# A longer ring for gathered V rows, U slots released by twos and a third index buffer in a PEER block on one core

## What is computed

```python
def _peer(h, w_peer_q, peer_sub_keys, peer_u, peer_v):
    q = (h @ w_peer_q).reshape(B, S, PEER_HEADS, 2, PEER_HALF)
    s = jnp.einsum('bshcd,hcnd->bshcn', q, peer_sub_keys)
    top_s, top_i = lax.top_k(s, PEER_TOPK)              # 16 of 128, twice
    ...                                                 # 16 best of the 256 sums
    expert_idx = jnp.take_along_axis(cand_idx, best_pos, axis=-1)
    g = jax.nn.softmax(best_s, axis=-1)
    ...
    u = peer_u[ib]                                      # gather
    a = jax.nn.gelu(jnp.einsum('td,ted->te', hb, u), approximate=False)
    return jnp.einsum('te,ted->td', gb * a, peer_v[ib]) # gather
```

## Time and profile before

| | |
|---|---|
| median of 3 runs | 1005.27 us (998.52 to 1005.81) |
| the profiled execution | 1007.17 us |
| its span in the trace | 1005.4 us |
| mean granted clock of PE | 0.9 |
| busy: PE, DVE, POOL, ACT | 796.7, 605.9, 491.5, 192.4 us |
| the software DMA queue (the gathers) | 268.47 MB, 70.9% of 16 DMA engines' span |

### The profile page before, as it was taken

The page is one execution under the profiler, slowest core; times in us unless marked ns, Lnnn a source line. Parts: engine busy times, 40 slices in busy tenths (PEclk is TensorE's granted clock), DMA queues, the critical chain, the costliest instruction groups (busy, mean ns, idle before and its releaser), DMA issues.

```text
span 1005.4 us, 8411 instructions
## 1 busy us (share of the span) xinstructions
PE 796.7 (79%) x2726; PEld 463.6 (46%) x2726; DVE 605.9 (60%) x1359; ACT 192.4 (19%) x483; POOL 491.5 (49%) x529
## 2 busy tenths in 40 slices
PE   5999999999694769777696969696676859595764
PEld 5877588867352435334342524243333425252321
DVE  6245675236777575747557474848474665778455
ACT  1012122201313121213022112212120312212111
POOL 1000000000767566756666666666566666666662
PEclk9999999999797979988887979797988879797988
DMA  9998956582999999999999999999999999999994
GB/s 350 375 365 317 343 188 247 196 265 84 341 359 380 328 373 376 376 353 372 347 367 353 366 370 360 376 363 368 365 373 345 358 361 362 368 365 396 358 410 152
DMA packets 112282, 338.48 MB, mean 337 GB/s; under 512 B 9184, under 2 KB 20976, under 8 KB 112112
## 3 DMA queue, kind: packets, MB, share of 16 engines
q0 software_dynamic: 73728, 268.47, 70.9%
q1 hardware_dynamic: 35936, 67.11, 18.7%
q10 hardware_dynamic: 2576, 2.37, 0.8%
HBM read 336.87 MB, written 1.05 MB: 336 GB/s over the span
## 4 chain that ended last, share of the span: by engine, by line
POOL 36%; PE 29%; issue 18%; DVE 7%; another core or an unknown queue 6%; DMA 3%; ACT 1%; POOLq 0%; DVEq 0%; ACTq 0%
POOL ring L351 36%; PE bank L987 10%; PE bank L1159 6%; DVE ring L832 3%; PE bank L1090 3%; PE bank L980 3%; DMA ring<-in_peer_u_dram,small 1%; PE bank L1104 1%; PE h_ps L936 1%; PE bank L1123 1%; PE h_ps L953 1%; PE h_ps L941 1%; DMA ring<-in_peer_v_dram,small 1%; DMA x_sb<-in_x_dram 0%
## 5 line engine op out<-in xcount | busy, mean ns | idle before, releaser
L832 DVE CUSTOM_DVE_ANT_0 ring<-ring,h_ps 128x1024 f32<-128x1024 f32 x256 | 310.9, 1221 | 225.0 <-DMA ring<-in_peer_u_dram,small 203.4
L351 POOL DMA_INDIRECT ring<-in_peer_u_dram,small x256 | 247.5, 967 | 283.7 <-DVE small L813 203.5
L1159 PE MATMUL bank<-ring,small 128*128 128x512 f32 x512 | 258.4, 669 | 150.9 <-ACT small L519 87.2
L351 POOL DMA_INDIRECT ring<-in_peer_v_dram,small x256 | 240.0, 938 | 170.3 <-remote 89.0
L1159 PEld LDWEIGHTS bank<-ring,small 128*128 128x128 f32 x512 | 109.3, 217 | 290.5 <-issue 290.5
L1159 PE MATMUL bank<-ring,h_sb 128*128 128x512 f32 x500 | 225.1, 608 | 16.4 <-ACT h_sb L519 6.5
L1159 PEld LDWEIGHTS bank<-ring,h_sb 128*128 128x128 f32 x500 | 96.5, 196 | 135.5 <-issue 128.5
L987 PE MATMUL bank<-hT,ring 128*128 128x256 f32 x448 | 102.3, 389 | 1.1 <-ACT hT L402 1.1
L987 PEld LDWEIGHTS bank<-hT,ring 128*128 128x128 f32 x448 | 86.3, 194 | 16.3 <-issue 4.4
L1123 PE MATMUL bank<-hT,wpq 128*128 128x128 f32 x512 | 67.9, 288 | 17.6 <-issue 17.1
L1123 PEld LDWEIGHTS bank<-hT,wpq 128*128 128x128 f32 x512 | 65.1, 202 | 27.0 <-issue 26.4
(11 more groups left out here) (159 smaller groups left out, 515.8 us busy)
## 6 DMA issues: line engine op xcount, KB each, us to landing
ring<-in_w_cond_dram SPq DMA_DIRECT2D x10, 2048.0 KB, 13.8
ring<-in_w_in_dram SPq DMA_DIRECT2D x8, 2048.0 KB, 12.3
wpq<-in_w_peer_q_dram SPq DMA_DIRECT2D x8, 1024.0 KB, 12.0
ring<-in_w_cond_dram SPq DMA_DIRECT2D x4, 1024.0 KB, 14.5
ring<-in_w_out_dram SPq DMA_DIRECT2D x2, 2048.0 KB, 10.7
ring<-in_peer_u_dram,small POOLq DMA_INDIRECT x256
ring<-in_peer_v_dram,small POOLq DMA_INDIRECT x256
ring<-in_w_in_dram SPq DMA_DIRECT2D x2, 1024.0 KB, 13.5
```

What stands on the lines that cost most here:

```text
L351: nc.gpsimd.indirect_dma_start(out=dst[e], out_offset=None, in_=table[0], in_offset=bass.IndirectOffsetOnAxis(ap=idx[:, k:k + 1], axis=0)) ...
L832: V.tensor_tensor_reduce(u_ring[e], u_ring[e], h_ps[:], 1.0, 0.0, ALU.mult, ALU.add, acol[:, g, e:e + 1]).then_inc(dots_done, 1)
L1159: last = T.matmul(bank[ACC_BANKS[t][m]][:], diag_of(p, g)[:, e, :], v_ring[e][:, m * BLK:(m + 1) * BLK], start=False, stop=end, skip_group ...
```

## The change

`v_ring` gets five more slots, the two rows of `ln1` and three rows of `cond`, so it has 13. The first 16 V rows (groups 0 and 1) use slots 0 to 7 as before; from row 16 on, row j goes to slot (j - 8) % 13. Tables worked out in Python give each row its slot (`V_SLOT`), how many rows that slot had before (`V_TURN`, for the landing semaphores) and the last row before it in the slot (`V_BEFORE`, for the wait on `v_used`). Row 16 waits for the end of the second tile's norm. The U slots are released two by two: ahead of U rows 0, 2, 4 and 6 POOL waits for two dot products of the group before (`dots_done`), where before it waited once for all eight. `idx` has three buffers of 16, so the write of the indices of pair p waits for the V rows of pair p - 3. The order in which the gathers are issued, their number and size stay as they are, and so does all that DVE, ACT and PE compute.

```diff
+VROWS_LATER = GROUP + 5
+V_ROWS = 2 * PAIRS * GROUP
+V_SLOT = [j % GROUP if j < 2 * GROUP else (j - GROUP) % VROWS_LATER for j in range(V_ROWS)]
+V_TURN = [V_SLOT[:j].count(V_SLOT[j]) for j in range(V_ROWS)]
+V_BEFORE = [max((i for i in range(j) if V_SLOT[i] == V_SLOT[j]), default=-1) for j in range(V_ROWS)]
...
-        idx = small[:, 2870:2902].bitcast(U32)
+        idx = small[:, 2870:2918].bitcast(U32)
...
+        v_ring += [ln1[:, 0, :], ln1[:, 1, :], cond[:, GT1, :], cond[:, SH2, :], cond[:, SC2, :]]
...
-        v_in = [sem(f"v_in{i}") for i in range(GROUP)]
+        v_in = [sem(f"v_in{i}") for i in range(VROWS_LATER)]
...
-                pool.wait_ge(idx_ready, p + 1)
-                for g in range(2):
-                    n = 2 * p + g
-                    first = a * TOPK + g * GROUP
-                    pool.wait_ge(dots_done, GROUP * n + GROUP)
-                    for e in range(GROUP):
-                        gather(peer_u, u_ring, e, first + e, u_in)
-                    for e in range(GROUP):
-                        if e % 2 == 0:
-                            pool.wait_ge(v_used, GROUP * n + e + 2)
-                        gather(peer_v, v_ring, e, first + e, v_in)
+            def u_row(n, e):
+                if e == 0 and n % 2 == 0:
+                    pool.wait_ge(idx_ready, n // 2 + 1)
+                if n == 0:
+                    if e == 0:
+                        pool.wait_ge(dots_done, GROUP)
+                elif e % 2 == 0:
+                    pool.wait_ge(dots_done, GROUP * n + e + 2)
+                gather(peer_u, u_ring[e], n, e, u_in[e])
+
+            def v_row(n, e):
+                j = GROUP * n + e
+                if e % 2 == 0:
+                    before = max(V_BEFORE[j], V_BEFORE[j + 1])
+                    pool.wait_ge(v_used, GROUP + max(before + 1, 0))
+                if j == 2 * GROUP:
+                    pool.wait_ge(h2_ready, 2 * TILES)
+                gather(peer_v, v_ring[V_SLOT[j]], n, e, v_in[V_SLOT[j]])
+
+            for n in range(2 * PAIRS):
+                for e in range(GROUP):
+                    u_row(n, e)
+                for e in range(GROUP):
+                    v_row(n, e)
...
-                if not (isinstance(p, int) and p == 0):
-                    dve.wait_ge(v_used, p * TOPK - TOPK + GROUP)
-                V.scalar_tensor_tensor(out=idx[:, a * TOPK:(a + 1) * TOPK], in0=sel[:, 0:TOPK], scalar=float(NKEYS),
+                if p >= 3:
+                    dve.wait_ge(v_used, GROUP + (p - 2) * TOPK)
+                V.scalar_tensor_tensor(out=idx[:, p % 3 * TOPK:(p % 3 + 1) * TOPK], in0=sel[:, 0:TOPK], scalar=float(NKEYS),
...
-                        pe.wait_ge(v_in[e], 16 * (n + 1))
+                        j = GROUP * n + e
+                        pe.wait_ge(v_in[V_SLOT[j]], 16 * (V_TURN[j] + 1))
...
-                            last = T.matmul(bank[ACC_BANKS[t][m]][:], diag_of(p, g)[:, e, :], v_ring[e][:, m * BLK:(m + 1) * BLK],
+                            last = T.matmul(bank[ACC_BANKS[t][m]][:], diag_of(p, g)[:, e, :], v_ring[V_SLOT[j]][:, m * BLK:(m + 1) * BLK],
```

More of the change, by code:

```diff
@@ L368, in _, with gather @@
-            for i in range(0, PAIRS // 2):
-                gather_pair(i, 0)
-                gather_pair(i, 1)
+            def gather(table, dst, n, e, landed):
+                p = n // 2
+                k = p % 3 * TOPK + n % 2 * GROUP + e
+                nc.gpsimd.indirect_dma_start(
+                    out=dst, out_offset=None, in_=table[0],
+                    in_offset=bass.IndirectOffsetOnAxis(ap=idx[:, k:k + 1], axis=0)).then_inc(landed, 16)
+            def u_row(n, e):
[7 more added lines that the diff above has]
+                gather(peer_u, u_ring[e], n, e, u_in[e])
@@ L861, in own_rows @@
                 for e in DVE_ROWS:
-                    dve.wait_ge(v_in[e], 16 * (n + 1))
+                    j = GROUP * n + e
+                    dve.wait_ge(v_in[V_SLOT[j]], 16 * (V_TURN[j] + 1))
                     if e == DVE_ROWS[0]:
-                        link(V.tensor_scalar(base, v_ring[e], wts[:, 1, e:e + 1], None, ALU.mult))
+                        link(V.tensor_scalar(base, v_ring[V_SLOT[j]], wts[:, 1, e:e + 1], None, ALU.mult))
                     else:
-                        link(V.scalar_tensor_tensor(out=base, in0=v_ring[e], scalar=wts[:, 1, e:e + 1], in1=base,
+                        link(V.scalar_tensor_tensor(out=base, in0=v_ring[V_SLOT[j]], scalar=wts[:, 1, e:e + 1], in1=base,
                                                     op0=ALU.mult, op1=ALU.add))
```

## The result

| | before | changed kernel |
|---|---|---|
| median, side by side | 1004.92 us (998.52 to 1005.81, 4 runs) | 1045.28 us (1029.84 to 1051.48, 4 runs) |
| ratio to before | | 1.0317, 95% interval 1.0199 to 1.0435 |
| the profiled execution, its span | 1007.17, 1005.4 us | 1029.84, 1028.1 us |

The change makes the kernel about 3% slower (2.0 to 4.4% by the interval); 948 us was predicted, 5.9% faster. The profiled execution is the fastest of the four, so its rows show the loss at its smallest: 1028.1 - 1005.4 = 22.7 us of span.

A forecast was written before the change was run, and what follows sets the result against it. POOL's pauses starving DMA and a PE loop were taken as bounds; afterwards the loop sets the pair: 308.0 + 14.72 pairs x 42.1 (619.7) + 18.9 = 946.6 us of span, so 948 us, range 935 to 962 (915 to 990 with rivals 1 and 2).

The forecast's parts named there:

- What bounds the kernel now: Gather stage from 308 us: POOL's pauses on V slots hold DMA to 365 GB/s, where stretches reach 411 to 412.
- rival 3: Whole kernel: no change, about 1003 us, as the 46.3 us loop stays or memory gives only 365 GB/s; chance 0.13.
- Five more V slots: POOL's waits on `v_used`: taken as gone, with 9.4 us slack and 0 to 1.2 us of pause left a pair.
- The loop over PE: From top-16 through V rows, query and scores to the next: 42.1 us a pair, longer than DMA's 40.7.
- They come together with POOL's pauses, so I take the small one: Query stalls on PE: 1.45 us too much a pair, out of 1.45 to 4.6, as they accompany POOL's pauses.
- rival 4: Slower: POOL's pauses let PE's counts through; without them scores' counts lag 10.6 us, loop 49.3 us, 1054 us; chance 0.10.
- U slots by twos: POOL's waits on `dots_done` ahead of U rows: worth 0 now; without it, up to 2 us a pair lost.
- Third index buffer: Index write on DVE behind the top-16: worth 0; excludes a stall of up to 8.9 to 10.6 us.
- The first 308 us stay, and the tail: Start and end: the first 308.0 us unchanged, and 18.9 us from the last gather to the end of the span.
- Rival 1: Gather stage: lag and stalls vanish with the pauses and DMA sets the pair at 1.272 us a gather, 928 us; chance 0.19.

The follow-up runs named there:

- A with 8 KB rows: The kernel before the change with 256 gathers of 8 KB rows in place of 512 of 4 KB, fetching the neighbouring row for a second expert: 918.00 us, ratio 0.9148.

## Why the prediction was wrong, point by point

- **What bounds the kernel now.** That DMA delivers 365 GB/s because POOL pauses, and 411 where it doesn't, was right. That 411 is no burst was right as well: 414 GB/s over 592 us in A with 8 KB rows. The 358 GB/s for one core, cited in rival 3, don't bind here, where one core runs alone. The Trainium skill has the number for such a core elsewhere (HBM Reference, Specifications (TRN2)): a core that streams alone measures about 425 GB/s. The 414 to 416 GB/s of the runs lie 2 to 3% under it.
- **Five more V slots: wrong too, as a consequence.** "I take the V wait as gone and count the lag in the loop below." The V waits of POOL are still some 91 us from 310 to 985 us (the five rows above that aren't on L848; 93.8 before), because V rows are used later. The slack of 9.4 us was worked out for a pair of 40.7 us; pairs now take 49.3 us in the mean of twelve, from 39.3 to 62.6 (worked out from the starts of the top-16s).
- **The loop over PE, term by term.** Means over eleven pairs of the changed kernel's timeline, from the top-16 at 376.9 to that at 906.0 (the pair before these, with a query of 23.2 us, makes the twelve). From its start to the query: 20.3 us (4.2 + 15.4 + 0.8 = 20.4 predicted, 20.2 before). The query: 6.9 (5.05; 5.8 before). To the first V matmul of the second group: 1.2 (0). The eight V rows until the scores: 16.4 (13.9). The scores' matmuls 0.6, lag until ACT saves them 2.2 (1.95; 4.4 before), and to DVE 0.4. Sum 48.1 against 42.1. That the lag came out near the 1.95 us predicted is luck: it was under 0.1 us in eight of the eleven pairs and 4.5, 6.5 and 13.3 in three. Most of the loss is where I had put nothing: the second V group begins late and is stretched, 3.7 us together, behind waits for its diagonals (L535) and waits for which the profile has no releaser; and the query has 1.8 more, or 3.2 with the twelfth pair. In the pairs where nothing was late the loop took 39.3 and 39.7 us: the 37.9 us of work proper were well read.
- **"They come together with POOL's pauses, so I take the small one": the step that failed.** This is the assumption under the loop of 42.1 us, which measured 48.1. In the earlier trace rows the stall in the query and the lag stand beside a pause, and I read the pause as their cause. The runs show the opposite order: lateness comes of gathers issued back to back (none of 33 queries stalled behind 12 or fewer in 20 us, 30 of 31 behind 15 or more), and in a pause the held counts come through. The trace of before had the sign for it, since the pauses ended 3 to 4 us after they began however long ago PE had used the row, and rival 4 said so.
- **Rival 4, 0.10.** The sign and the place (counts late while POOL issues without a pause) were right and its 1054 us is nearer to the medians than any other case; its form was not, as the mean lag of the scores fell, and it named a queue running low as what lets the counts through. That a pause lets them through is borne out by the bursts; that the queue must run low is not, since DMA at a share of 1.01 goes without lateness and at 0.59 with it. Its counter-argument, that row 6 often passed without a pause while DMA was full, was no argument, since it said nothing of POOL's pace.
- **U slots by twos: "worth 0 now".** Right alone (0.9963). Beside the ring and the index buffer they are worth 80 us, by the ratios (1.1114 - 1.0317, of 1005). "If it weren't there, up to 2 us a pair" was too low: once DVE is late, POOL's single wait for eight products makes the next U rows late and closes a second loop.
- **Third index buffer: 0.** Right alone (1.0006, 0.9971 to 1.0040), and 2.9 hundredths dearer beside the ring, for a reason that stays open.
- **The first 308 us stay, and the tail.** V row 0 of group 2 is issued at 308.13 (308.03 before), and from the last gather, at 1009.55, to the end it is 18.5 us (18.9 predicted).
- **Rival 1** comes out where the gathers are half as many: A with 8 KB rows takes 918 us (928 by rival 1), with 40.5 us a pair.

**What stays open.** Why indirect gathers issued closer than about 1.45 us apart make the counts and the short instructions of PE, DVE and ACT late by 3 to 20 us isn't settled. Excluded as causes are bytes, row transfers, full DMA engines, the longer ring by itself and POOL's being busy. The instruction fetches, 22 and 20 packets in the whole trace, are too few. What stays with the number of gathers at any size is its 16 updates on landing, 12.9 a us at 1.24 us and 11.0 at 1.46, and whatever else GpSimd does for each. A third candidate is the recording of the trace itself, as each timed execution here was recorded. For it speak the missing updates, that matmuls inside a query stall though only the last of them updates a semaphore, and that stalls begin only behind 14 or more short matmuls; no run told the three apart. If it is the recording, the change could do without it what was predicted. Nor was a pattern tried that keeps the mean pace at 1.45 us and places the gaps where no engine needs the rows.

No kernel of the study that computes the whole layer beats the one before by more than the 0.4% of the U slots by twos.

## What to carry to other kernels

Before taking away the waits of an engine that issues many small indirect gathers, look at whether the other engines' counts are late already (a wait that ends 3 us and more after its releaser's last work, single short matmuls with idle time that nothing explains): the pauses may be what they live on. Count the gathers in the 20 us before each late one, not the mean over the stage, and look at whether updates are missing from the trace, since the recording is not ruled out as the cause. Then count gathers, not bytes: fewer and larger ones gave 8.5% (in a kernel that fetches the neighbour in place of a second expert; to use it, rows that are needed together must lie together), where more buffers lost 3%. And a wait for a whole group's slots is free only as long as nothing in the loop is late.

## What the runs showed of the hardware

- One indirect gather costs POOL 1.24 to 1.25 us from issue to issue, with 2, 4 or 8 KB rows, and 1.20 us with 64 rows in place of 128.
- 256 gathers of 128 x 8 KB read 414 to 416 GB/s for 592 us; 512 gathers of 4 KB never held more than 365 over the stage.
- At 1.24 to 1.33 us from gather to gather, in recorded executions of this kernel, a query of 32 matmuls took up to 23 us in place of 3.73 (24.4 with 2 KB rows), stalling behind its 14th to 31st matmul, mostly in multiples of 0.7 us (0.71, 1.42, 2.1, 2.8 and 3.5 us in the timeline); the top-16 of the stretch shown took 7 us more. At 1.46 us both were undisturbed, with POOL busy for 88% of the time.
- In the stalls the recorded updates of semaphores of all engines and landings come one every 0.70 us, and then in a burst (14 in half a microsecond in the one shown).
